# A softmax spread over two places and put ahead of the recurrence on VectorE, in a two-block transformer on one Trainium2 core

## What is computed

```python
def mixer(z, ...):
    h = z @ w_in
    (q_a, k_a, v_a, r_a, lr_f, lr_b, q_b, k_b, v_b, g_a, g_b) = jnp.split(h, SPLIT_POINTS, axis=-1)
    a = gla_branch(q_a, k_a, v_a, r_a, lr_f, lr_b, gla_w2, gla_b2, gla_gn)
    b = attention_branch(q_b, k_b, v_b, q_norm, k_norm, cos, sin)
    y = (sigmoid(g_a + b_merge[0]) * (a @ w_pa) + sigmoid(g_b + b_merge[1]) * (b @ w_pb))
    return y @ w_out

# gla_branch ends, per head (4 heads of 128 values) with the gated tile:
    o = o * lax.rsqrt(jnp.mean(o * o, axis=-1, keepdims=True) + EPS)
    return (o * gn_gain) * silu(r)
# attention_branch, per head (8 heads, 2 key heads) and block of 128 queries:
    p = softmax(q @ k.T);  o = p @ v
```

## Time and profile before

| | |
|---|---|
| median of 3 runs | 1908.04 us (1907.89 to 1908.21) |
| the profiled execution | 1907.37 us, its span 1906.1 us |
| TensorE busy | 1874.9 us, 98% of the span |
| VectorE busy | 1361.6 us, 71% |
| ScalarE busy | 1052.1 us, 55% |
| granted TensorE clock | 0.999 |

### The profile page before, as it was taken

One profiled execution on the slowest core, in us unless ns is written; L12 is line 12 of the kernel. 1 busy time (PEld: TensorE's weight loads), 2 busy tenths in 40 slices (PEclk: granted clock), 3 DMA queues, 4 the chain that ended last, 5 costly groups with the idle time before them and its releaser, 6 DMA issues.

```text
span 1906.1 us, 36604 instructions
## 1 busy us (share of the span) xinstructions
PE 1874.9 (98%) x15273; PEld 1832.3 (96%) x15273; DVE 1361.6 (71%) x2413; ACT 1052.1 (55%) x1786; POOL 1.3 (0%) x8
## 2 busy tenths in 40 slices
PE   7999999999999999999999999999999999999998
PEld 6999998899999999999889999999999999999998
DVE  5777666577776677667668777698787559887844
ACT  6444565655444544456566545576565457656642
POOL 0000000000000000000000000000000000000000
PEclk9999999999999999999999999999999999999999
DMA  6776332346775577633235777444455544444553
GB/s 251 265 271 251 129 142 92 112 165 237 258 285 205 199 261 269 240 133 133 90 138 190 278 283 286 150 149 158 173 187 180 193 176 150 155 177 178 188 188 111
DMA packets 51812, 365.93 MB, mean 192 GB/s; under 512 B 6620, under 2 KB 8060, under 8 KB 9920
## 3 DMA queue, kind: packets, MB, share of 16 engines
q1 hardware_dynamic: 51648, 363.59, 52.4%
HBM read 362.52 MB, written 1.05 MB: 191 GB/s over the span
## 4 chain that ended last, share of the span: by engine, by line
PE 89%; DVE 6%; ACT 3%; DMA 1%; issue 1%; SPq 0%; DVEq 0%; ACTq 0%
PE bank L423 26%; PE bank L424 26%; PE bank L425 26%; DVE w_lo L1511 2%; PE bank L459 1%; PE bank L455 1%; PE bank L456 1%; ACT w_hi L1001 1%; DVE full L1553 1%; PE bank L693 1%; PE bank L621 1%; DVE xn_lo L1517 1%; PE bank L678 1%; DMA raw_b<-in_weights 0%; PE bank L723 0%
## 5 line engine op out<-in xcount | busy, mean ns | idle before, releaser
L423 PE MATMUL bank<-xn_hi,w_hi 128*128 128x272 f32 (+2 forms) x2624 | 758.7, 289 | 1.2 <-DVE w_lo L1511 1.2
L425 PE MATMUL bank<-xn_lo,w_hi 128*128 128x272 f32 (+2 forms) x2624 | 748.8, 285 | 0.0
L424 PE MATMUL bank<-xn_hi,w_lo 128*128 128x272 f32 (+2 forms) x2624 | 747.4, 285 | 0.0
L423 PEld LDWEIGHTS bank<-xn_hi,w_hi 128*128 128x128 f32 x2624 | 494.3, 188 | 9.7 <-issue 5.5
L424 PEld LDWEIGHTS bank<-xn_hi,w_lo 128*128 128x128 f32 x2624 | 494.6, 189 | 1.1
L425 PEld LDWEIGHTS bank<-xn_lo,w_hi 128*128 128x128 f32 x2624 | 494.8, 189 | 0.0
L1511 DVE TENSOR_TENSOR w_lo<-raw_b,w_hi 128x1024 fp32r<-128x1024 f32 (+1 forms) x282 | 356.4, 1264 | 145.1 <-ACT w_hi L1001 144.4
L1511 DVE TENSOR_TENSOR w_lo<-raw_a,w_hi 128x1024 fp32r<-128x1024 f32 (+1 forms) x282 | 356.1, 1264 | 142.5 <-ACT w_hi L1001 141.9
L1001 ACT ACTIVATE w_hi<-raw_a 128x1024 fp32r<-128x1024 f32 (+1 forms) x282 | 307.0, 1090 | 254.3 <-PE bank L425 226.5
L1001 ACT ACTIVATE w_hi<-raw_b 128x1024 fp32r<-128x1024 f32 (+1 forms) x282 | 306.9, 1089 | 249.2 <-PE bank L425 232.7
L425 PE MATMUL bank<-h_lo,w_hi 128*128 128x272 f32 (+1 forms) x704 | 201.8, 287 | 0.0
(11 more groups left out here) (319 smaller groups left out, 2830.0 us busy)
## 6 DMA issues: line engine op xcount, KB each, us to landing
raw_a<-in_weights SPq DMA_DIRECT2D x123, 1024.0 KB, 4.6
raw_b<-in_weights SPq DMA_DIRECT2D x123, 1024.0 KB, 4.6
ada_raw<-in_ada_w SPq DMA_DIRECT2D x48, 1024.0 KB, 4.8
raw_a<-in_weights SPq DMA_DIRECT2D x16, 1408.0 KB, 5.7
raw_b<-in_weights SPq DMA_DIRECT2D x16, 1408.0 KB, 5.8
c_rows<-in_c_rows SPq DMA_DIRECT2D x3, 512.0 KB, 3.6
raw_a<-in_weights SPq DMA_DIRECT2D x2, 768.0 KB, 3.9
raw_b<-in_weights SPq DMA_DIRECT2D x2, 768.0 KB, 4.0
```

The costliest lines, as they stand in the source:

```text
L423: pe.matmul(o, wh, xh, start=start, stop=False)
L424: pe.matmul(o, wl, xh, start=False, stop=False)
L425: return pe.matmul(o, wh, xl, start=False, stop=stop)
```

## The change

On VectorE, a softmax step is cut in two: `maxima` stays in the place of the scores, `probabilities` goes to the next place, with the low part `b_lo` of an output. From place 16 on VectorE alone takes the chains in the opposite order, attention ahead of the recurrence. The high part `a_hi` of a gated tile (ScalarE) and its low part `a_lo` (VectorE) go one place later, ahead of the next tile's root. Lists of TensorE, SP and GpSimd are as before.

```diff
@@ -1188,21 +1188,28 @@
         def square(h):
             act.activation(c.sq[:, live], bank[2 + h % 2][:, live], ACT.Square).then_inc(*k.up("gla_a", ("square", l, h)))
 
+        def high(h):
+            act.wait_ge(*k.at("gla_v", ("gated", l, h)))
+            act.activation(c.a_hi[:, h, live], c.full[:, 0, live], ACT.Copy).then_inc(*k.up("x_hi", ("a", l, h)))
+
         for p in range(2):
+            if p:
+                high(1)
             yield
             act.wait_ge(*k.at("gla_mm", ("o", l, p)))
             square(2 * p)
             yield
             for h in (2 * p, 2 * p + 1):
+                if h % 2:
+                    high(h - 1)
                 act.wait_ge(*k.at("gla_mm", ("sum", l, h)))
                 if h:
                     act.wait_ge(*k.at("gla_v", ("normed", l, h - 1)))
                 inverse_root(c.gate[:, 0, live], bank[4][:, live], 1.0 / GLA_DV, "gla_a", ("root", l, h))
                 if h % 2 == 0:
                     square(h + 1)
-                act.wait_ge(*k.at("gla_v", ("gated", l, h)))
-                act.activation(c.a_hi[:, h, live], c.full[:, 0, live], ACT.Copy).then_inc(*k.up("x_hi", ("a", l, h)))
                 yield
+        high(3)
 
     def attention(l):
         b_s, b_t, b_o = 5, 6, 7
@@ -1744,6 +1751,8 @@
                 yield
         live = LIVE[l]
         for p in range(2):
+            if p:
+                low(c.a_lo[:, 1, live], c.full[:, 0, live], c.a_hi[:, 1, live], ("a", l, 1))
             dve.wait_ge(*k.at("gla_mm", ("att", l, p)))
             for d in range(2):
                 for j in range(2):
@@ -1756,6 +1765,8 @@
             yield
             for h in (2 * p, 2 * p + 1):
                 f = c.full[:, 0, live]
+                if h % 2:
+                    low(c.a_lo[:, h - 1, live], f, c.a_hi[:, h - 1, live], ("a", l, h - 1))
                 dve.wait_ge(*k.at("gla_a", ("root", l, h)))
                 if h:
                     dve.wait_ge(*k.at("x_lo", ("a", l, h - 1)))
@@ -1764,9 +1775,8 @@
                 dve.wait_ge(*k.newest("gla_v"))
                 dve.scalar_tensor_tensor(out=f, in0=f, scalar=c.half[:, 16 + h:17 + h], in1=c.r_act[:, h, live], op0=ALU.mult,
                                          op1=ALU.mult).then_inc(*k.up("gla_v", ("gated", l, h)))
-                dve.wait_ge(*k.newest("gla_v"))
-                low(c.a_lo[:, h, live], f, c.a_hi[:, h, live], ("a", l, h))
                 yield
+        low(c.a_lo[:, 3, live], c.full[:, 0, live], c.a_hi[:, 3, live], ("a", l, 3))
 
     def attention(l):
         b_s, b_t, b_o = 5, 6, 7
@@ -1802,33 +1812,41 @@
                                          op1=ALU.mult).then_inc(*k.up("att_v", ("scaled", l, j - 1)))
             yield
 
-        def softmax(step, js, bs):
-
-            stats = [c.stat[:, 4 * (2 * (step % 2) + j):4 * (2 * (step % 2) + j) + 4] if step != "meta" else c.stat[:, 0:4] for j in js]
-            for j, b, s in zip(js, bs, stats):
+        def heads(step, bs):
+
+            return [(j, b, c.stat[:, 4 * (2 * (step % 2) + j):4 * (2 * (step % 2) + j) + 4] if step != "meta" else c.stat[:, 0:4])
+                    for j, b in enumerate(bs)]
+
+        def maxima(step, bs):
+            for j, b, s in heads(step, bs):
                 dve.wait_ge(*k.at("att_mm", ("score", l, step, j)))
                 dve.reduce_max(s[:, 0:1], bank[b][:, 0:T], AX).then_inc(*k.up("att_v"))
                 dve.wait_ge(*k.newest("att_v"))
                 dve.tensor_scalar(s[:, 1:2], s[:, 0:1], -HD ** -0.5, None, ALU.mult).then_inc(*k.up("att_v", ("max", l, step, j)))
-            for j, s in zip(js, stats):
+
+        def probabilities(step, bs):
+
+            for j, _, s in heads(step, bs):
                 dve.wait_ge(*k.at("att_a", ("exp", l, step, j)))
                 dve.reciprocal(s[:, 3:4], s[:, 2:3]).then_inc(*k.up("att_v"))
                 dve.wait_ge(*k.newest("att_v"))
                 dve.tensor_scalar(c.prob[:, j, :], c.prob[:, j, :], s[:, 3:4], None, ALU.mult).then_inc(*k.up("att_v", ("prob", l, step, j)))
 
         if live == TA:
-            softmax("meta", (0,), (b_s,))
-            yield
+            maxima("meta", (b_s,))
+            yield
+            probabilities("meta", (b_s,))
             yield
         for step in range(8):
-            softmax(step, (0, 1), (b_s, b_t))
+            maxima(step, (b_s, b_t))
+            yield
+            probabilities(step, (b_s, b_t))
             if step and step % 2 == 0:
                 p = step // 2 - 1
                 low(c.b_lo[:, p, live], bank[b_o][:, live], c.b_hi[:, p, live], ("b", l, p))
             yield
-            yield
+        yield
         low(c.b_lo[:, 3, live], bank[b_o][:, live], c.b_hi[:, 3, live], ("b", l, 3))
-        yield
 
     def mixer(l):
         u0, stage, live = FIRST["mix", l], ("mix", l), LIVE[l]
@@ -1876,7 +1894,7 @@
                 m = at - 42
                 dve.wait_ge(k.sem["unit_done"], u + 1)
                 dve.tensor_tensor(c.x[:, m, live], c.x[:, m, live], bank[m % 4][:, live], ALU.add).then_inc(*k.up("tile_v", ("res", l, m)))
-            step(chains, at)
+            step(chains if at < 16 else chains[::-1], at)
             if at < 49:
                 split_lo(u + 4)
             if at >= 42:
```

## The result

The changed kernel takes 1920.27 us (1920.09 to 1920.89), the kernel before 1907.97 us: 12.3 us more, a ratio of 1.0064 (1.0051 to 1.0077). The forecast was 1923, range 1916 to 1928.

A forecast was written before the change was run, and what follows sets the result against it. TensorE, busy 98% of the span, was taken as the bound, so its waits are paid in full. Second mixer +6.2 us and first +9.1 us gave +15.3 on 1907.4, or 1922.7, forecast as 1923; range 1916 to 1928 (8 in 10).

The forecast's parts named there:

- The cause: VectorE's softmax places: prob stands behind w_lo, which waits for ScalarE's w_hi behind the exponentials; together +15.3 us.
- R: Undisturbed step of the second mixer: first prob is ready 5.31 us after the scores start; longer at some places.
- The second head: Turns on TensorE: VectorE makes the second head's prob some 0.55 us after the first, costing 0.3 us more a step.
- The places: Turns of both mixers, each priced with its own cover on TensorE: second mixer +6.2 us, first +9.1 us.
- the case's own +11.5 to +18: Whole kernel: bounds in us of the summed terms, giving 1919 to 1926; the forecast had 82 in 100.
- Places 23 and 27 of the second mixer: Turns that waited 2.2 us before: the removed wait is replaced by one of the same size, change taken as 0.
- the 0.36 us at 28: Second mixer, place 28: a score's wait for pt goes, since ScalarE no longer waits for gated; -0.4 us.
- The waits in the profile: TensorE's turns: some 12 of 17 wait for prob, about 15 to 18 us in all, the longest 1.4 to 2 us.
- The gain not had: Softmax stretches: old waits removed and nothing in their place, about -2.6 us, 1905; 2 in 100.
- The clock rival: TensorE after waits of 1.4 us or more: restarts at half pace, 8 us more, 1931; 3 in 100.
- The price of 1.3 us for a slow restart: TensorE after 10.71 us of idle: first 13 matmuls at half pace cost 13 x 0.1 = 1.3 us.
- rows 9: Profile rows cited for the first 13 matmuls after 10.71 us of idle, read as 0.22 us apart, then 0.125.

The follow-up runs named there:

- one operation more: Changed kernel with one unused 256-column add (0.42 us) on VectorE behind the w_lo of each of the nine score places; 1928.67 us, ratio 1.0104.
- three operations more: Changed kernel with three unused 256-column adds (0.42 us each) on VectorE behind the w_lo of each of the nine score places; 1949.79 us, ratio 1.0213.
- the kernel of place 17 with `w_lo` behind `prob`: Changed kernel with w_lo behind the next place's probabilities and VectorE's chains reversed from place 19 on, not 16; 1909.12 us, ratio 1.0005.

## Why the prediction was right, and where it was off

- **The cause.** Right. Moving `w_lo` behind `prob` gave back the 12 us, moving `w_hi` ahead of the exponentials 9.7, making the softmax whole 12. The later gated parts alone were 2 us faster than before, and with the reversal and a whole softmax the time was that of before.
- **R, the time from scores to `prob`.** Forecast 5.31, measured 988.36 + 0.36 - 983.50 = 5.22, and TensorE took it up 0.06 later, at 5.28. The reciprocal starts at 988.17, 1.15 after `w_lo`, whose 1.23 I had counted in full, and `prob` 0.11 after the end of that `w_lo`, not 0.2.
- **The second head.** The charge of 0.3 us was the term that was mis-sized most. At place 31 of the second mixer scores to output went from 979.66 - 972.52 = 7.14 to 992.51 - 983.50 = 9.01, 1.87 more. The turn came 5.28 - 3.57 = 1.71 later after the scores and took 0.96 in place of 0.81, 0.15 more; together 1.86. So a second head costs 0.15 where I had charged 0.3. The trace of before had a hint: the two turns that waited there, at places 23 and 27, took 1.03 us and not 0.81 (the row shows only three of the six transposes), so 0.2 rather than 0.3. The mechanism (it is the second head that sets the end) was confirmed. Over 13 steps this is 2 us of the 3.6 that the sum was too high.
- **The places.** Place 17: 1.3 in the first mixer (from 292.50 to the scores of place 18) and 1.7 in the second, for 1.4 and 2.1. Place 19 of the second: 1.1 for 1.2. Place 31 there: 1.9 for 2.0. Place 33 of the first: 1.4 for 1.8. Before, the product behind that turn started 0.79 us after it, against 0.57 at place 31 of the second mixer, right behind the end of ScalarE's move of a bank; now it is 0.72 at both, so the longer turn cost nothing more there. Places 27 and 31 of the first: 0.1 and 0.3 for 0.5 each. First mixer 7.2 for 9.1, second 4.5 for 6.2. The misses nearly all went one way, and the result lies at the lower end of the case's own +11.5 to +18.
- **Places 23 and 27 of the second mixer.** As forecast, their waits did not go but changed their cause: 0.44 in place of 0.55 us at 23 and 1.51 in place of 1.64 at 27. Both places were some 0.2 us shorter than before, where I took 0, and the 0.36 us at 28 went.
- **The waits in the profile.** 12 of the 17 turns waited, as forecast, but for 11.7 us in all and not 15 to 18: the longer turns are part of the price and not of the waits, and the price was too high. The longest were 1.50, 1.51 and 1.54 us at places 17, 27 and 31 of the second mixer; place 33 of the first had 1.32 where 1.4 to 2 was forecast.
- **The gain not had.** Right in size: removing what waits there was worth 2 us with the gated parts alone and 3.6 with the reversal from place 19 as well.
- **The clock rival.** Rightly small here: with waits of up to 1.54 us the granted clock was 1.00 in every softmax stretch. It was not empty: with one operation more, the stretch from 960 to 1000 us, with waits of 1.84 and 1.87 us, was granted 0.91, part of the time at the 1.2 GHz level. The Trainium skill ("TensorE: Matmul & The Clock Gate", section "A second HAM failure mode: psum-queue depth-cycling") has such a fall from short, frequent idles in another kernel; the kernels with one and three operations more and the one with the split alone show a fall with short waits at many turns, the changed kernel does not. The price of 1.3 us for a slow restart was one execution's: rows 9 are 12 gaps of 0.24 us and not 13 of 0.22, and in the changed kernel's trace the slow pace lasted long enough to cost 1.2 us more.

## What to carry to other kernels

When a step is cut in two and its second half goes "one place later", ask what the place ends with: here every place ended with a split of weights that waits for another engine, and the half that was moved for slack ended up behind it. Price the new chain from its first link to the waiting engine and compare it with what that engine does meanwhile; the difference is paid in full where that engine is the bound. And take a change of several parts apart: one part of this one was worth 2 us and, with another part from a later place on, 3.6 us, while the third cost 12 on top of them and 58 alone. What a part costs depends on what else is in.

## What the runs showed of the hardware that was not expected

- Stretches in which TensorE waited at several turns, up to 1.54 us at a time (the changed kernel), were granted 1.00 all through. With waits of 1.84 and 1.87 us the stretch from 960 to 1000 us was granted 0.91, and stretches of the split alone, with their longer waits (up to 4.0 us), 0.85 to 0.91; some of the turns there took 1.22 to 1.45 us in place of 0.96. Not every such wait did this: in the kernel with one operation more, the wait of 1.84 us at 918.79 left the clock at 1.00 from 880 to 960 us. Nor does it take many: in the kernel of place 17 with `w_lo` behind `prob` the only wait for `prob` in the second mixer was the one of 1.86 us at 910.31, and behind it the clock fell:

```profile
910.00:920.00 10.00, 9.69 (x72) 8.68 (x74) 5.61 (x14) 4.06 (x11) 0.00 (x0) 0.83 0.31 107
```

- What is left of the loss beyond the waits themselves is 20 of 58 us with the split alone and 9 of 28 us with three operations more. Which waits bring the fall was not settled.
- Before the first changed place the lists are the same in all kernels, and still the meta scores started anywhere from 291.09 to 292.94 us in the thirteen traces. Part of this is the slow pace at the start: TensorE did 55 and 56 matmuls in the first 20 us in the two traces with the earliest scores, and 45 to 48 in six of those after 292.3. Part is a lower clock in the stretch from 20 to 60 us, which was granted 0.91, 0.96 or 1.00. Differences of a microsecond between two executions say nothing here; the medians and the starts within a stretch do.
